# First attention of a two-block transformer kernel: order of a gate unit, copies in halves, silu of the convolution, modulation tiles

## The reference, cut to what matters

```python
mod = silu(c) @ ada_w[layer] + ada_b[layer]         # shift, scale, gate: "modulation"
h = modulate(rmsnorm(x, norm_g), shift, scale)
k, v, q, za, glu, zb = split(h @ w_in)
q, k = rope(rmsnorm(q)), rope(rmsnorm(k))           # 8 query heads, 2 key heads, head size 128
p = softmax(q k_all^T * HEAD_DIM ** -0.5)           # 256 queries x 512 keys (latent and context)
attn = p @ v_all
conv = silu(layernorm(depthwise_conv(a * sigmoid(b)), ln_g, ln_b))
mix = concat([attn * silu(za), conv * silu(zb)])
x = x + gate * (mix @ ev_w_out)
```

## Time and profile before

| | |
|---|---|
| runs, us | 2953.44, 2955.72, 2956.95 (median 2955.72) |
| profiled execution, span, us | 2956.1; no other time is listed for it |
| PE, PEld busy | 90%, 70% |
| DVE, ACT, POOL busy | 73%, 21%, 30% |
| HBM traffic | 929 MB read, mean 316 GB/s |
| first attention, from scores(0) to the unit after the last values | 329.1 to 449.1 us |
| `ev_out`, first to last unit | 469.8 to 583 us |

### The profile page before, as it was taken

The page is one execution under the profiler, slowest core; times in us unless marked ns, Lnnn a source line. Parts: engine busy times, 40 slices in busy tenths (PEclk is TensorE's granted clock), DMA queues, the critical chain, the costliest instruction groups (busy, mean ns, idle before and its releaser), DMA issues.

```text
span 2956.1 us, 31045 instructions
## 1 busy us (share of the span) xinstructions
PE 2663.8 (90%) x11792; PEld 2070.4 (70%) x11792; DVE 2160.4 (73%) x2978; ACT 607.8 (21%) x1271; POOL 894.0 (30%) x712
## 2 busy tenths in 40 slices
PE   6999889999999999999999999667676758999997
PEld 5888678866587588478657688667666755666665
DVE  6787476577896747524677769999999878656667
ACT  1121240110110110122000021122377776000000
POOL 1100001000000100000000024777767657656664
PEclk8999999999999999999999999888877779999998
DMA  9954469868787834324978769999999988999998
GB/s 402 421 190 153 152 226 409 352 247 355 287 319 300 311 128 143 142 100 153 361 279 321 268 273 416 421 421 421 413 421 421 403 338 283 403 410 414 414 414 349
DMA packets 147736, 935.12 MB, mean 316 GB/s; under 512 B 16400, under 2 KB 16656, under 8 KB 53136
## 3 DMA queue, kind: packets, MB, share of 16 engines
q0 software_dynamic: 101376, 604.02, 51.1%
q1 hardware_dynamic: 44784, 320.66, 28.0%
q10 hardware_dynamic: 1440, 8.59, 0.7%
HBM read 929.02 MB, written 4.19 MB: 316 GB/s over the span
## 4 chain that ended last, share of the span: by engine, by line
PE 58%; DMA 19%; DVE 8%; ACT 7%; POOL 5%; issue 3%; DVEq 0%; SPq 0%; ACTq 0%
PE G L579 32%; PE M L894 7%; DMA acc<-v_rows,proj 6%; PE B L894 3%; DMA mix<-v_rows,proj 3%; DMA vec<-peer_u,proj 3%; ACT vec L1576 2%; DMA aring<-peer_u,proj 2%; PE M L1162 2%; DMA proj<-v_rows,proj 2%; DVE vec L2512 2%; PE G L894 2%; POOL aring L551 1%; PE G L1150 1%; POOL acc L563 1%
## 5 line engine op out<-in xcount | busy, mean ns | idle before, releaser
L579 PE MATMUL G<-h,ring 128*128 128x256 f32 x3264 | 715.6, 380 | 0.5 <-ACT h L1298 0.2
L579 PEld LDWEIGHTS G<-h,ring 128*128 128x128 f32 x3264 | 616.1, 190 | 91.6 <-issue 6.8
L536 POOL DMA_DIRECT2D aring<-ada x176 | 93.2, 530 | 1493.7 <-DVE mods L1707 1445.4
L1707 DVE CUSTOM_DVE_ANT_0 aring<-aring,acc,vec 128x2048 f32<-128x2048 f32 x160 | 372.2, 2350 | 49.9 <-DMA aring<-ada 46.8
L579 PE MATMUL G<-proj,ring 128*128 128x256 f32 x1472 | 322.1, 380 | 0.9 <-DVE proj L2324 0.9
L579 PEld LDWEIGHTS G<-proj,ring 128*128 128x128 f32 x1472 | 279.6, 191 | 41.4 <-issue 3.4
L1209 PE MATMUL M<-sq,mix 128*128 128x512 f32 x688 | 301.4, 594 | 0.0
L551 POOL DMA_INDIRECT aring<-peer_u,proj x130 | 228.6, 1759 | 197.2 <-DVE dots L2484 83.3
L1209 PEld LDWEIGHTS M<-sq,mix 128*128 128x128 f32 x688 | 203.6, 297 | 89.3 <-ACT mix L1590 0.7
L2512 DVE SCALAR_TENSOR_TENSOR vec<-acc,dots,vec 128x1024 f32<-128x1024 f32 x149 | 191.5, 1285 | 97.1 <-DMA acc<-v_rows,proj 91.8
L2484 DVE CUSTOM_DVE_ANT_0 aring<-sq,aring 128x2048 f32<-128x2048 f32 x104 | 236.4, 2290 | 29.1 <-DMA aring<-peer_u,proj 18.7
(11 more groups left out here) (494 smaller groups left out, 3670.5 us busy)
## 6 DMA issues: line engine op xcount, KB each, us to landing
ring<-weights SPq DMA_DIRECT2D x219, 1024.0 KB, 5.3
aring<-ada POOLq DMA_DIRECT2D x176, 1024.0 KB, 8.6
sq<-v_blocks SPq DMA_DIRECT2D x43, 1024.0 KB, 8.0
proj<-v_blocks SPq DMA_DIRECT2D x21, 1024.0 KB, 8.0
ring<-first SPq DMA_DIRECT2D x16, 896.0 KB, 11.2
sq<-ada POOLq DMA_DIRECT2D x8, 1024.0 KB, 20.9
acc<-ada POOLq DMA_DIRECT2D x4, 1024.0 KB, 19.4
proj<-ada POOLq DMA_DIRECT2D x4, 1024.0 KB, 22.9
```

What stands on the lines that cost most here:

```text
L536: pool.dma_start(ada_at(n), ada[n]).then_inc(ada_in[ada_slot(n)], 16)
L579: mm = nc.tensor.matmul(bank[:, 0:TOK], lhsT=ring[:, slot, weights_at + t * P:weights_at + (t + 1) * P], rhs=rhs[:, t, :], start=(t == ord ...
L1707: V_.tensor_tensor_reduce(out=tile, in0=tile, in1=vector, scale=1.0, scalar=bias, op0=ALU.mult, op1=ALU.add, accum_out=column).then_inc(ad ...
```

## The change

Five edits, all in the first attention and the stretch behind it. PE does unit ez(4) between scores(0) and scores(1); only ez(5) stays behind the values of head 0. The transposes signal `pt_done` twice a head, after four and after eight; ACT copies 512 columns at each signal, and PE starts the values with the first half and waits for the second one before the third of four key tiles. `turned_through` gives the new counts of the two semaphores; the second attention (nk = 2) waits for the same events as before. ACT does `conv_silu` after the copies of head 7 and before it takes out zb(5) to zb(7). Of the modulation tiles of group 1 that DVE did in and around head 7, three fewer stand before the first product with the convolution gate: 3 in `waiting` and 2 in `between` become 0 and 2, the 4 between the products become 6, and the 6 before piece 0 become 7.

```diff
--- before.py
+++ after.py
@@ -191,6 +191,11 @@
     put("lower", (rows >= HEADS) & (rows < 2 * HEADS))
     put("minus_lower", -1.0 * ((rows >= HEADS) & (rows < 2 * HEADS)))
     return t
+
+
+def turned_through(base, heads):
+
+    return 2 * HEADS + heads if base else 2 * heads
 
 
 def on_pe(n):
@@ -720,7 +725,7 @@
                     mm = nc.tensor.matmul(M[:, j * w:(j + 1) * w], lhsT=C("rot"), rhs=s, start=True, stop=True)
                 mm.then_inc(rot_done, 1)
 
-            def attention(base, nk, q_of, k_of, v_of, pt, extra, between={}, copying={}):
+            def attention(base, nk, q_of, k_of, v_of, pt, extra, between={}, copying={}, first_wait=None):
 
                 w = nk * P
 
@@ -740,23 +745,32 @@
                     mm.then_inc(s_done, 1)
 
                 scores(0)
+                if first_wait is not None:
+                    first_wait()
                 for hh in range(HEADS):
                     if hh + 1 < HEADS:
                         scores(hh + 1)
                     pe.wait_ge(p_ready, base + hh + 1)
                     if base + hh > 0:
-                        pe.wait_ge(pt_copied, base + hh)
+                        pe.wait_ge(pt_copied, turned_through(base, hh))
                     for kt in range(nk):
                         for qt in range(2):
                             mm = nc.tensor.transpose(M[:, 1024 + kt * 256 + qt * P:1024 + kt * 256 + (qt + 1) * P],
                                                      att[:, qt * w + kt * P:qt * w + (kt + 1) * P], ident)
+                        if nk == 4 and kt == 1:
+                            mm.then_inc(pt_done, 1)
                     mm.then_inc(pt_done, 1)
                     if hh in copying:
                         copying[hh]()
-                    pe.wait_ge(pt_copied, base + hh + 1)
+                    if nk == 4:
+                        pe.wait_ge(pt_copied, 2 * hh + 1)
+                    else:
+                        pe.wait_ge(pt_copied, turned_through(base, hh + 1))
                     if base + hh >= 2:
                         pe.wait_ge(o_read, base + hh - 1)
                     for kt in range(nk):
+                        if nk == 4 and kt == 2:
+                            pe.wait_ge(pt_copied, 2 * hh + 2)
                         mm = nc.tensor.matmul(O[hh % 2][:, 0:TOK], lhsT=v_of(hh, kt),
                                               rhs=pt[:, kt * 256:(kt + 1) * 256], start=(kt == 0), stop=(kt == nk - 1))
                     mm.then_inc(pv_done, 1)
@@ -870,8 +884,8 @@
             attention(0, 4, lambda hh: proj[:, hh, :], lambda hh: kv_keys[:, hh // 4, :],
                       lambda hh, kt: vtok[:, kt * 256 + (hh // 4) * P:kt * 256 + (hh // 4 + 1) * P],
                       sq[:, 2048:3072], False,
-                      {0: lambda: ez(4, 2), 1: ez_and_mean, 2: lambda: ez(7), 3: ez_after_mean, 4: zb_and_variance,
-                       5: zb_after_variance, 6: lambda: zb(4), 7: lambda: zb(5, 3)})
+                      {0: lambda: ez(5), 1: ez_and_mean, 2: lambda: ez(7), 3: ez_after_mean, 4: zb_and_variance,
+                       5: zb_after_variance, 6: lambda: zb(4), 7: lambda: zb(5, 3)}, first_wait=lambda: ez(4))
             dense("ev_out", [proj], first=0, count=4, coming=[(mix_ready, 1, range(0, 14)), (mix_ready, 2, range(14, 16))])
             dense("ev_out", [proj], first=4, count=10)
             residual_sum(sq, 0, 1)
@@ -1318,7 +1332,7 @@
                 def exps(hh):
                     act.wait_ge(nmax_ready, base + hh + 1)
                     if base == 0 and hh > 0:
-                        act.wait_ge(pt_done, base + hh)
+                        act.wait_ge(pt_done, turned_through(base, hh))
                     for qt in range(2):
                         src = M[:, qt * w:(qt + 1) * w] if nk == 4 else att[:, qt * w:(qt + 1) * w]
                         nc.scalar.activation(att[:, qt * w:(qt + 1) * w], src, ACT.Exp, bias=small[:, 2 + qt:3 + qt],
@@ -1326,10 +1340,18 @@
 
                 exps(0)
                 for hh in range(HEADS):
-                    act.wait_ge(pt_done, base + hh + 1)
-                    if hh > 0:
-                        act.wait_ge(pv_done, base + hh)
-                    nc.scalar.activation(pt, M[:, 1024:1024 + nk * 256], ACT.Copy).then_inc(pt_copied, 1)
+                    if nk == 4:
+                        act.wait_ge(pt_done, 2 * hh + 1)
+                        if hh > 0:
+                            act.wait_ge(pv_done, hh)
+                        nc.scalar.activation(pt[:, 0:512], M[:, 1024:1536], ACT.Copy).then_inc(pt_copied, 1)
+                        act.wait_ge(pt_done, 2 * hh + 2)
+                        nc.scalar.activation(pt[:, 512:1024], M[:, 1536:2048], ACT.Copy).then_inc(pt_copied, 1)
+                    else:
+                        act.wait_ge(pt_done, turned_through(base, hh + 1))
+                        if hh > 0:
+                            act.wait_ge(pv_done, base + hh)
+                        nc.scalar.activation(pt, M[:, 1024:1024 + nk * 256], ACT.Copy).then_inc(pt_copied, 1)
                     if hh + 1 < HEADS:
                         exps(hh + 1)
                     if hh in between:
@@ -1414,13 +1436,13 @@
                 zb(2)
                 std(CONV_T * P, count=2, bank=G[1])
 
-            def zb_and_conv():
-                zb(4)
+            def conv_and_zb():
                 conv_silu()
+                zb(5, 3)
 
             softmax_steps(0, 4, sq[:, 2048:3072], HD ** -0.5,
                           {0: lambda: ez(4, 2), 1: lambda: ez(6), 2: lambda: ez(7), 3: lambda: ez(8), 4: zb_and_std,
-                           5: lambda: zb(3), 6: zb_and_conv, 7: lambda: zb(5, 3)})
+                           5: lambda: zb(3), 6: lambda: zb(4), 7: conv_and_zb})
 
             act.dma_start(att[:, 0:1024], wsT).then_inc(spatial_in, 16)
             act.dma_start(att[:, 1024:2048], bs.partition_broadcast(P)).then_inc(spatial_in, 16)
@@ -1758,7 +1780,7 @@
                     s = M[:, 0:2 * w].rearrange("p (a b) -> p a b", a=2)
                     if base:
                         if hh:
-                            dve.wait_ge(pt_done, base + hh)
+                            dve.wait_ge(pt_done, turned_through(base, hh))
                         step(tt(probs, s, C("mask").rearrange("p (a b) -> p a b", a=2), ALU.add))
                         s = probs
                     step(V_.tensor_reduce(small[:, 0:2], s, AX, ALU.max))
@@ -2041,14 +2063,14 @@
             softmax(0, 4, HD ** -0.5, gate_attention, 
                     {0: lambda: ada_part(0, 2, 1), 1: lambda: ada_part(0, 4, 1), 2: conv_centre,
                      3: lambda: ada_part(0, 8, 1), 4: lambda: ada_part(0, 10, 1), 5: conv_scale,
-                     6: lambda: ada_part(0, 14, 1), 7: lambda: ada_part(1, 3, 2)},
+                     6: lambda: ada_part(0, 14, 1), 7: lambda: ada_part(1, 0, 2)},
                     {0: lambda: ada_part(0, 0, 2), 1: lambda: ada_part(0, 3, 1), 2: lambda: ada_part(0, 5, 2),
                      3: lambda: ada_part(0, 7, 1), 4: lambda: ada_part(0, 9, 1), 5: lambda: ada_part(0, 11, 2),
-                     6: lambda: ada_part(0, 13, 1), 7: lambda: (ada_part(0, 15, 1), ada_part(1, 0, 3))})
+                     6: lambda: ada_part(0, 13, 1), 7: lambda: ada_part(0, 15, 1)})
             dve.wait_ge(conv_act, CONV_T)
             dve.wait_ge(unit_evac, UNIT0["zb"] + 4)
             step(tt(conv[:, 0:6, :], conv[:, 0:6, :], proj[:, 32:38, :], ALU.mult), on=mix_ready)
-            ada_part(1, 5, 4)
+            ada_part(1, 2, 6)
             dve.wait_ge(unit_evac, UNIT0["zb"] + 6)
             step(tt(conv[:, 6:8, :], conv[:, 6:8, :], proj[:, 38:40, :], ALU.mult), on=mix_ready)
 
@@ -2116,7 +2138,7 @@
                 dve.wait_ge(unit_done, middle_unit(name) + 8)
                 step(tt(c21, c21, p4, ALU.add), on=halves_made)
 
-            ada_part(1, 9, 6)
+            ada_part(1, 8, 7)
             add_residual("ev_out", 0)
             ada_part(1, 15, 1)
             ada_part(2, 0, 7)
```

## The result

The changed kernel takes 2938.91 us (median of four runs, 2938.20 to 2940.28) against 2954.58 us of the kernel before in the same series: ratio 0.9943, 95% interval 0.9930 to 0.9957, that is 12.7 to 20.7 us less. The prediction was 2948.4 us with a range from 2941 to 2954: the way was right, the size was half, and the range did not hold it.

What follows compares the result with a forecast made beforehand. PE was taken as the bound, then the DMA stream behind the attention. Gains of 5.7 + 3.6 + 5.6 = 14.9 us, less 6.2 of wait and 1.4 of clock, gave 7.3 us off the profiled span: 2948.4 us, range 2941 to 2954.

Steps and rivals of the forecast that it cites:

- Head 0, 5.7 us: Head 0: with ez(4) in PE's hole behind scores(0), at the upper clock, scores(2) start 5.7 us earlier.
- Halves, 0.86 us a head: Each head: copies in halves let values start 1.29 us after the transposes instead of 2.15, 0.86 us less.
- Heads 3 and 6 wait for DVE: Transposes of heads 3 and 6 wait for DVE's division, giving back 0.81 and 0.75 us; heads 1 to 6 gain 3.6.
- Head 7, 5.6 us: Head 7: without conv_silu ahead of the copy, zb(5) starts 3.12 us after the transposes instead of 8.72, 5.6 us less.
- In that full stream three missing MB cost 12.4 us: Modulation stream behind the attention: three later refills of 1 MB, 4.15 us each, delay it 12.4 us.
- PE's wait of 6.2 us: At residual piece 2, before ev_out's last unit: PE waits 6.2 us, the stream's 12.4 less 6.2 of cover.
- a cover of 6.2 us: Residual piece 2 ends at 567.85 us, PE asks for it at 574.08, so 6.2 us of delay cost nothing.
- The 1.4 us for the lower clock: Behind the 6.2 us wait of PE: a hole of that length brings the lower clock, costing 1.4 us.
- The second product: Product with six tiles now ahead of it: PE would wait 2.6 us, absorbed in the later wait, adding nothing.
- No wait at all: Rival: the modulation stream follows PE, missing tiles cost under 6.2 us, and the time is 2940.8 us; chance 0.08.
- two tiles short: Rival: two tiles short, not three; PE waits 2.1 us, the clock stays, 2942.9 us; chance 0.17.
- 5 us for a tile of 1 MB: Second product: a tile beside a weight chunk gets half of 421 GB/s, landing in 5 us, so no wait there.

Runs made afterwards that it cites:

- e1: The changed kernel with the modulation tiles in their old places, those of the kernel before: 2941.1 us, ratio 0.9956 to the kernel before.
- e5: From e1, three unused loads of 1 MB added, asked for by ACT at the end of the last zb unit: 2949.2 us, ratio 0.9981 to the kernel before.
- p4: The kernel before with only the modulation tiles moved as in the change: 2957.4 us, ratio 1.0009 to the kernel before.
- e3: The changed kernel with five instead of six tiles between the two products, eight instead of seven before piece 0: 2941.4 us, ratio 0.9953.
- e2: The changed kernel with two more modulation tiles deferred, none under between in head 7: 2950.5 us, ratio 0.9986 to the kernel before.
- e4_again: Second run of e1 with one tile moved from before head 3's division to head 1, one from before head 6's to head 4: 2935.1 us, ratio 0.9936.

## Why the prediction was wrong, point by point

- **Head 0, 5.7 us: right, with some luck.** Scores(2) start 22.1 us after scores(0), 27.9 before: 5.8 us. The unit did not keep the upper clock throughout (7.93 us instead of 6.99), but scores(0), which the change does not touch, took 2.83 us instead of 3.58. In the other profiles with both edits of PE scores(2) start between 20.4 and 23.5 us, a gain of 4.4 to 7.5.
- **Halves, 0.86 us a head: right.** 1.29 us from transposes to values in every head.
- **Heads 3 and 6 wait for DVE: right, with a misreading in head 6.** They gave back 0.9 and 0.4 us against 0.81 and 0.75. The division of head 6 in the kernel before:

```profile
428.46 0.49 DVE L1772 TENSOR_SCALAR att<-att,small 128x512 f32<-128x512 f32 x1
```

  It ends at 428.95 and the transposes start at 429.50, so with the 0.06 us between the two in head 3 it had 0.5 us to spare, not 0.1, and 0.86 - 0.49 = 0.37 was to be given back. Heads 1 to 6 gave 3.9 us for 3.6 (transposes of head 7 at 101.6 after 111.3, less 5.8).
- **Head 7, 5.6 us: right** to the hundredth, 3.12 us from transposes to zb(5).
- **"In that full stream three missing MB cost 12.4 us ... I take three": this step failed.** Counted from zb(5), PE's own position, the last tile ends 9.4 us later than before (124.5 for 115.1), not 12.4. The deferral makes 6.7 us of it, and 2.7 are there without it (e1, 117.8): the stream followed PE by 11.2 us of 13.9. The prediction had the whole 12.4 from the deferral and nothing from the second part. The tiles were asked for later, but the DMA engines were not idle for all of that time: 1.3 MB were lost beside e1, not three. That the number of MB was the only thing wrong is not shown: an extra MB costs the 4.1 us charged (e5), but in p4 all three were lost and cost 8.6 us.
- **PE's wait of 6.2 us was 2.9**, in two pieces, which goes with a cover of 6.2 us and a delay of 9.4. **The 1.4 us for the lower clock fell away**, since behind neither piece did the last unit slow down; where it did (e3, e5, e2) it cost 1.2 to 1.5 us. With these two the working gives 7.3 + 3.3 + 1.4 = 12.0 us, and od is 12.4 us earlier in the trace.
- **The second product** was late by 1.7 us where 2.6 was worked out, and it was absorbed as stated: e3 moved the wait and won nothing.
- **The rivals.** "No wait at all" (2940.8, chance 0.08) came nearest by the time, but it was not what happened: e1 shows what no wait looks like. By the mechanism "two tiles short" came nearest: a wait of 2.1 us and the clock stays (2942.9, chance 0.17).
- **What stays open.** The failed step, with the clock that hung on it, is 4.7 us of the miss. Put right, the working leads to some 2943 to 2944 us, inside the range; the measured 2938.9 lies outside, and that part of the miss is not explained by it. 1.1 us of it is the lower median of the kernel before in its series (2954.6 for 2955.7). Three profiles of the changed kernel are 12.1 to 12.9 us ahead at od, and 12.0 to 16.6 at the end, against the one of before. The medians differ by 15.7 us, and the interval begins at 12.7. From od to the end, where all kernels do the same apart from three waits in e5, the fourteen profiles take 2362.2 to 2370.7 us, and the one of before 2366.6. So no gain behind od is shown, and some 3 us of the 15.7 may be scatter.

The prediction cited the Trainium skill, "DMA: Bandwidth & Descriptors", section on queues, rings and completion order: engines go round between their queues. From an even share it estimated 5 us for a tile of 1 MB, and no wait at the second product. The trace has a DMA wait of 4.74 us for the sixth tile and 1.67 us for PE, so the measurement decides against that estimate. The load of the fifth tile, issued at 441.82, did land within 5.3 us, and that of the sixth, issued at 444.09, took 11.2. So the estimate holds for one and not for the other, and whether the rule itself holds is not shown by either.

## What to carry to other kernels

When a change defers requests to a stream that is full later, count the bytes that the engines really leave unused in the emptier stretch, not the requests moved: three requests were 1.3 MB in the changed kernel and 3.1 MB in p4. The bytes bound the delay only roughly (2.8 to 5.2 us for an MB here). A hole that was taken out of PE moved the DMA stream by less than PE here (11.2 of 13.9 us), so look for the next point at which the two meet, and keep its cover. Two short waits can be cheaper than one long one, if the lower clock comes behind the long one (one profile of e3 against three of the changed kernel). Before two single profiles are compared, take out stretches that differ in the same program, such as head 0 here: without that the extra MB of e5 seems to cost 3.6 us and not 4.1.

## What the runs showed of the hardware that was not expected

- **Head 0 comes in three lengths.** From the start of scores(0) to that of scores(1), with the unit between, six profiles have 10.4 us, two 11.8 and two 8.7. At 8.7 everything runs at the upper clock, though PE had been idle for 2.4 us before the scores in each of them. PE of e4_again:

```profile
325.31 1.95 PE L737 MATMUL M<-sq,proj 128*128 128x512 f32 x4 [2.40 <-DVE sq L1772]
327.10 7.07 PE L584 MATMUL G<-h,ring 128*128 128x256 f32 x32
334.01 1.88 PE L737 MATMUL M<-sq,proj 128*128 128x512 f32 x4
```

  The same program thus differs by up to 3.1 us in one place, a fifth of the whole effect of the change.
- **Length of a PE wait and the clock behind it.** After 1.87 us (p4) and after 0.9 to 1.8 us (changed kernel, three profiles) the last unit took 3.62 us; after 2.89, 8.36 and 9.11 us it took 5.06, 5.16 and 4.80. The granted clock at its beginning was 1.00 in the changed kernel and 0.50 in these three (e3: 558.5 to 560 us).
- **An MB of DMA that nobody reads costs another stream 4.1 us** (counted from zb(5)) when the engines are full, and not its own 2.5 us (e5). That the weights go on taking their share while the stream catches up would explain it, but it was not measured by itself.
